# Layer 1's experts in a fused two-block model: tokens picked and results added by one-hot products instead of gathers and scatters

## The chip, the cores and the metric

The kernel runs on one core of a Trainium2 chip. The metric is the device time of one launch in microseconds. Everything is computed in f32. Engines: PE is TensorE (matrix products, accumulating in 8 PSUM banks of 128 x 512 f32), PEld its loads of the stationary operand, DVE is VectorE, ACT is ScalarE, POOL is GpSimd, SP only issues DMAs.

## The reference

256 tokens and 256 context tokens of width 1024 go through two layers of a first block (attention branches, gated merge, then a mixture of experts), and the 256 tokens through a second block (linear attention, short convolution, dilated attention, feed-forward). In layer 1 (the last of the first block) only the 256 tokens have experts. What matters here is the mixture:

```python
def hier_moe(x, w_group, b_group, w_router, b_router, w_gate, w_up, w_down):
    # x: 256 tokens in layer 1. One of 4 groups, then 2 of its 8 experts for each token
    top_w = softmax(top_l) * g_w              # a weight for each of the two
    ...
    def expert_block(args):                   # w_gate, w_up: 1024x512, w_down: 512x1024
        hdn = jax.nn.silu(xb @ w_gate[e]) * (xb @ w_up[e])
        return hdn @ w_down[e]
    ...
    return segment_sum(ys[dest] * w_sorted[:, None], order // TOP_K, num_segments=t)

h = h + gt2 * y.reshape(b, n_lat, D_MODEL)
```

32 experts of 3 x 2 MB of weights each make 201 MB per layer. In layer 1 they get 16 tokens each on average. A block has CAP = 64 places; tokens beyond that go into further blocks, which are run only if there are any.

## The kernel before, in words

**Weights.** SP issues all weight loads in one queue, in the order in which they are used. Each is a block of 128 x 4096 f32 (2,097,152 bytes) in one of eight slots: four of a ring, and four "homes" (parts of `branches`, `heads`, all of `xT`, all of `values`) that are free while experts run. A load waits until TensorE has read the slot's block before (`expert_read`). So SP is up to eight blocks ahead. The last two blocks come in four pieces each.

**Layout of an expert.** All 128 columns of TensorE are used for 64 tokens by halving the other side: rows 0 to 63 of a bank hold the first half of the outputs, rows 64 to 127 the second. `up_product` (L1342 in its loop) makes the gate product into S[b] and the up product into V[b], 16 products each of a stationary 128x64 tile of tokens on 256 columns of weights; the two halves go to different columns of the array. `down_product` (L1354) has 8 products on 512 columns. The b alternates from expert to expert, and so do nearly all buffers.

**Tokens.** ScalarE stores the normed tokens xn2 in DRAM (x_rows, L2126). For expert e+2 GpSimd gathers 64 half rows twice into `xg` by the table `token_of`; TensorE turns them with 4 transposes into A[1] (L1331), ScalarE copies that to `xgT`. Expert 0's tokens come without DRAM, by one-hot products (`first_rows`, L1318). The tables come from one-hot products too (`place_rows`, L1307).

**Hidden rows and result.** ScalarE takes silu of the gate product, VectorE multiplies by the up product (L3051), TensorE turns the hidden rows with 2 transposes into A[0], ScalarE copies them to `hidT`, the down product goes to V[2+b], VectorE scales it by the gate gt2 into `y_sb` (L3118), and GpSimd scatters it to y_rows in DRAM. The last two experts' results (`KEPT_EXP`) are kept in SBUF (`last_y`, L3110) and added by one-hot products that also hold the tokens' weights (`last_sum`, L892). At the end y_rows is read back, one row pair per token (`result`, `first_result`), weighed (`weigh_first`, L3155) and added to `h` together with the banks of `last_sum` (`combine`, L3165). Then `second_in` does two norms (L3189 to L3209), turns the rows (L1459) and starts the second block's first products (L1493).

**Order.** `turn` runs eight experts (`MOE_AHEAD`); the first and the last eight are written out, the middle 16 are two passes of a hardware loop on every engine. Between the loop and the last eight stand the further blocks: each engine steps over them one by one if there are none. In experts 1 to 5 of the first eight VectorE also counts and lists the further blocks and places the kept ones. TensorE's order for an expert is: gate product, up product, transposes of the next expert's tokens, transposes of the hidden rows, down product. `keep_going` (L1278) are products without use that keep TensorE busy.

**Around it.** Ahead of the experts stand `merge_out` (the attention part's last product with the norm and the router's logits, L1225 to L1252) and `route`: VectorE picks the experts, TensorE ranks the tokens in each expert (L1289 to L1292).

## Time and profile before

| | |
|---|---|
| median of 3 runs | 2649.85 us (2649.2 to 2654.93) |
| profiled execution, its own time | 2650.99 us |
| its span, first to last instruction | 2649.1 us |
| PE busy | 2451.3 us, 93% |
| PEld busy | 1568.9 us, 59% |
| DVE / ACT / POOL busy | 960.6 / 434.9 / 170.1 us |
| granted TensorE clock, mean | 0.993 |
| DMA | 666.63 MB, mean 252 GB/s |
| layer 1's experts | gate product of expert 0 at 1532.28 us, last down product from 1998.05 us |

Times are read on the span's own clock, in microseconds from its first instruction. A MATMUL group's time reaches to the modelled end of its last instruction, which overlaps the next group: for a pace, starts are compared with starts. An f32 product shows as two MATMULs, a transpose as one. "[0.69 <-ACT ...]" behind a group is the idle time before it and what ended it; "issue" means nothing that the profile shows.

### The profile page before, as it was taken

The numbers are of one execution on the slowest core, as the hardware profiler recorded it, in microseconds if no ns is written. First come the engines' busy times: TensorE is split into PE (matmuls) and PEld (weight loads), VectorE is DVE, ScalarE is ACT, GpSimd is POOL, SyncE is SP. The second block draws the span as 40 slices with busy tenths as digits, with TensorE's granted clock in tenths as the row PEclk, the third lists the DMA queues.
The fourth block names the chain that finished last, engine by engine and source line by source line (L and its number), as shares of the span: only waits on it lengthen the run. The fifth ranks groups of instructions, "written<-read, shape, count | busy, mean of one in ns | idle before, by whom it ended". The sixth has DMA issues, their size and how long they took to land.

```text
span 2649.1 us, 32934 instructions
## 1 busy us (share of the span) xinstructions
PE 2451.3 (93%) x13288; PEld 1568.9 (59%) x13288; DVE 960.6 (36%) x1959; ACT 434.9 (16%) x1040; POOL 170.1 (6%) x193
## 2 busy tenths in 40 slices
PE   8999999999987777799999999777879999999998
PEld 4444455565554444447878755434445778997983
DVE  2695454335311111156555421000003333554750
ACT  2121223201100000022132110000001222211110
POOL 0000000000111111100000012111110000000000
PEclk9999999999999999999999999999999999999999
DMA  8365010434999999965424699999996333344441
GB/s 334 146 259 199 32 65 32 159 127 188 410 425 426 425 427 425 418 270 222 190 96 159 253 399 421 424 425 426 425 419 245 138 117 114 126 158 161 163 172 48
DMA packets 63062, 666.63 MB, mean 252 GB/s; under 512 B 13058, under 2 KB 13346, under 8 KB 24400
## 3 DMA queue, kind: packets, MB, share of 16 engines
q1 hardware_dynamic: 48384, 634.68, 59.3%
q0 software_dynamic: 13392, 24.82, 2.5%
q10 hardware_dynamic: 1152, 5.24, 0.5%
q8 instruction: 97, 1.59, 0.2%
q14 instruction: 37, 0.30, 0.0%
HBM read 664.28 MB, written 21.02 MB: 259 GB/s over the span
## 4 chain that ended last, share of the span: by engine, by line
PE 71%; DMA 25%; ACT 1%; issue 1%; DVE 1%; SPq 0%; POOL 0%; DVEq 0%; ACTq 0%; POOLq 0%
DMA ring<-in_w_moe 11%; DMA values<-in_w_moe 8%; PE act_bank L822 5%; PE act_bank L835 5%; PE act_bank L1484 5%; PE vec_bank L1016 4%; PE vec_bank L1225 4%; PE score_bank L1000 4%; PE score_bank L1342 4%; PE vec_bank L1354 3%; PE vec_bank L1000 3%; PE score_bank L1172 3%; PE vec_bank L1342 3%; DMA xT<-in_w_moe 3%; PE act_bank L1172 2%; PE act_bank L1493 2%
## 5 line engine op out<-in xcount | busy, mean ns | idle before, releaser
L3051 DVE TENSOR_TENSOR heads<-work,vec_bank 128x256 f32<-128x256 f32 x64 | 26.9, 421 | 505.6 <-PE vec_bank L1342 505.6
L822 PE MATMUL act_bank<-ring,xT 128*128 128x512 f32 x352 | 154.6, 593 | 3.2 <-ACT work L1827 2.5
L1354 PE MATMUL vec_bank<-ring,heads 128*64 128x512 f32 x512 | 116.9, 597 | 28.1 <-DMA ring<-in_w_moe 18.5
L1342 PE MATMUL score_bank<-ring,branches 128*64 128x256 f32 x1024 | 120.8, 389 | 23.1 <-DMA ring<-in_w_moe 11.3
L1342 PE MATMUL vec_bank<-ring,branches 128*64 128x256 f32 x1024 | 119.0, 385 | 24.9 <-DMA ring<-in_w_moe 24.7
L835 PE MATMUL act_bank<-xT,ring 128*128 128x512 f32 (+1 forms) x384 | 138.6, 521 | 0.0
L1484 PE MATMUL act_bank<-xT,ring 128*128 128x256 f32 x576 | 126.6, 380 | 0.6 <-ACT work L2247 0.6
L1342 PEld LDWEIGHTS score_bank<-ring,branches 128*64 128x64 f32 x1024 | 80.7, 140 | 71.6 <-issue 41.0
L1016 PE MATMUL vec_bank<-branches,ring 128*128 128x256 f32 (+1 forms) x416 | 122.7, 445 | 0.0
L1484 PEld LDWEIGHTS act_bank<-xT,ring 128*128 128x128 f32 x576 | 108.7, 190 | 16.7 <-issue 2.2
L1342 PEld LDWEIGHTS vec_bank<-ring,branches 128*64 128x64 f32 x1024 | 76.3, 138 | 65.6 <-DMA ring<-in_w_moe 29.9
L822 PEld LDWEIGHTS act_bank<-ring,xT 128*128 128x128 f32 x352 | 65.7, 190 | 82.9 <-issue 82.9
L3581 POOL TENSOR_TENSOR stat<-stat,const 128x1 f32<-128x1 f32 (+3 forms) x35 | 23.6, 673 | 1400.6 <-DVE stat L2727 465.1
L1225 PE MATMUL vec_bank<-ring 128*128 128x512 f32 x256 | 111.7, 593 | 0.0
L835 PEld LDWEIGHTS act_bank<-xT,ring 128*128 128x128 f32 x384 | 72.7, 190 | 63.7 <-issue 60.3
L2146 ACT ACTIVATE work<-score_bank 128x256 f32<-128x256 f32 x64 | 24.6, 384 | 519.3 <-PE score_bank L1342 482.9
L2471 DVE CUSTOM_DVE_ANT_0 ring<-ring,branches 128x1024 f32<-128x1024 f32 x80 | 100.6, 1279 | 19.8 <-DMA ring<-in_w_ada 19.6
L3629 POOL DMA_INDIRECT y_rows<-work,table x60 | 61.0, 1017 | 707.9 <-DVE work L3118 678.9
L1000 PE MATMUL score_bank<-xT,ring 128*128 128x256 f32 (+1 forms) x320 | 106.1, 472 | 0.0
L1016 PEld LDWEIGHTS vec_bank<-branches,ring 128*128 128x128 f32 x416 | 78.0, 190 | 35.6 <-issue 28.7
L1827 ACT ACTIVATE branches<-act_bank 128x512 f32<-128x512 f32 (+1 forms) x70 | 40.9, 585 | 303.8 <-PE act_bank L1331 287.0
L1354 PEld LDWEIGHTS vec_bank<-ring,heads 128*64 128x64 f32 x512 | 37.2, 136 | 87.2 <-issue 63.3
(535 smaller groups left out, 3885.2 us busy)
## 6 DMA issues: line engine op xcount, KB each, us to landing
ring<-in_w_moe SPq DMA_DIRECT2D x95, 2048.0 KB
ring<-in_w_in SPq DMA_DIRECT2D x29, 2048.0 KB
ring<-in_w_merge SPq DMA_DIRECT2D x27, 2048.0 KB
branches<-in_w_moe SPq DMA_DIRECT2D x24, 2048.0 KB
heads<-in_w_moe SPq DMA_DIRECT2D x24, 2048.0 KB
ring<-in_w_ada SPq DMA_DIRECT2D x23, 2048.0 KB
values<-in_w_moe SPq DMA_DIRECT2D x23, 2048.0 KB
xT<-in_w_moe SPq DMA_DIRECT2D x22, 2048.0 KB, 36.7
```

The costliest lines, as they stand in the source:

```text
L822: mm = pe.matmul(b.t[:, :], xT[:, k, tile * P:(tile + 1) * P], w[:, k * COLS:(k + 1) * COLS], start=(k == 0), stop=(k == KD - 1))
L835: mm = pe.matmul(b.t[:, 0:n], w[:, k * COLS + f * P:k * COLS + (f + 1) * P], xT[:, k, 0:n], start=(k == 0), stop=(k == KD - 1))
L1000: mm = pe.matmul(g.t[:, 0:n], merge_tile(l, i, MERGE_TILES * d + k), xs[:, k, 0:n], start=(k == 0), stop=(k == KD - 1))
L1016: mm = pe.matmul(y.t[:, 0:n], merge_tile(l, i, MERGE_TILES * d + KD + k), ys[:, BRANCH_ORDER[i], k, 0:n], start=(k == 0), stop=(k == 3))
L1172: mm = pe.matmul(b.t[:, 0:n], w[:, k, :], x[:, k, :], start=(first and k == 0), stop=(k == KD // 2 - 1), skip_group_check=True)
L1225: mm = pe.matmul(b.t[:, :], merged[l][:, k, tile * P:(tile + 1) * P], w[:, k * COLS:(k + 1) * COLS], start=(k == 0), stop=(k == KD - 1))
L1342: mm = pe.matmul(o.t[g * CAP:(g + 1) * CAP, 0:D_HALF], xgT[:, b, c, half * CAP:(half + 1) * CAP], w[:, c0:c0 + D_HALF], start=(k == 0), st ...
L1354: mm = pe.matmul(o.t[g * CAP:(g + 1) * CAP, :], hidT[:, b, c, half * CAP:(half + 1) * CAP], w[:, c0:c0 + HALF], start=(k == 0), stop=(k == 3))
L1484: mm = pe.matmul(b.t[:, 0:SEQ], w[:, k * COLS + f * P:k * COLS + (f + 1) * P], x2T[:, k, :], start=(k == 0), stop=(k == KD - 1))
L1493: mm = pe.matmul(b.t[:, :], x2T[:, k, tile * P:(tile + 1) * P], w[:, k * COLS:(k + 1) * COLS], start=(k == 0), stop=(k == KD - 1))
L2471: ins = nc.vector.tensor_tensor_reduce(ada_junk if k < ns - 1 else w, w, cond_rows[:, k, :], 1.0, bias, ALU.mult, ALU.add, dst)
L3629: pool.indirect_dma_start(out=half_rows(y_rows[l][0:tiles(l) * 2 * P, :]), out_offset=bass.IndirectOffsetOnAxis(ap=table[:, e:e + 1], axis=0),
```

## The change

Only layer 1 is touched (and what follows it at once). xn2 stays in SBUF, now in `h[:, 2:4]`, which is free there. For each expert VectorE compares every token's slot number with 1 to 64 (`find_tokens`, a one-hot matrix of 256 tokens x 64 places) and multiplies that by the token's weight (`hold_tokens`). TensorE makes the expert's transposed tokens as xn2^T x one-hot (`tokens_product`) into A[1]. It turns hidden rows and weighed one-hot together (`turn_held`), and adds y to all 256 tokens by 4 products into the four V banks, which accumulate over all 32 experts (`add_to_tokens`). These come one expert later, between the next up product and transposes. All buffers are single: S[0] for gate product and turned rows, S[1], A[0], A[1], `xgT[:, 0]`, `hid[:, 0]`, `y_sb[:, 0]`. x_rows, y_rows, the tables and the gathers, scatters and results of layer 1 go. The diff, cut:

```diff
-    xn2 = [xhat, ring[SUMS][:, 2048:4096].rearrange("p (t n) -> p t n", t=2)]
+    xn2 = [xhat, h[:, 2:4, :]]
...
+            if l == DEPTH - 1:
+                pe.wait_ge(A[1].free, A[1].fills)
+                pe.wait_ge(hot_made.sem, 1)
+                tokens_product(hot_now, A[1]).then_inc(A[1].full, A[1].fill())
+                mark["first_tokens"] = at_bank(A[1])
+                return
...
+        def tokens_product(hot, o):
+            for k in range(KD):
+                half, c = k // (KD // 2), k % (KD // 2)
+                for tile in range(2):
+                    mm = pe.matmul(o.t[:, c * P + half * CAP:c * P + (half + 1) * CAP], xn2[DEPTH - 1][:, tile, k * P:(k + 1) * P],
+                                   hot[:, tile, :], start=(k == 0 and tile == 0), stop=(k == KD - 1 and tile == 1),
+                                   skip_group_check=True)
+            return mm
+
+        def turn_held(o, hidden_, held_):
+            for c in range(2):
+                pe.transpose(o.t[:, c * P:(c + 1) * P], hidden_[:, c * P:(c + 1) * P], ident)
+            for tile in range(2):
+                mm = pe.transpose(o.t[:, (2 + tile) * P:(3 + tile) * P], held_[:, tile].rearrange("p h n -> p (h n)"), ident)
+            return mm
+
+        def add_to_tokens(y, turned_, first=False, last=False):
+            for tile in range(2):
+                for g in range(2):
+                    rows, b = slice(g * CAP, (g + 1) * CAP), V[2 * tile + g]
+                    mm = pe.matmul(b.t[:, :], turned_[rows, 2 * P + tile * P:2 * P + (tile + 1) * P], y[rows, :],
+                                   start=first, stop=last, skip_group_check=True)
...
+        def held_expert(q, e, loaded, first=False, second=False, final=False):
...
+            pe.wait_ge(A[1].free, A[1].fills)
+            for r, o in ((0, S[0]), (1, S[1])):
+                split = final and r == 1
+                if not split:
+                    pe.wait_ge(ring_loaded[s[r]], loaded(r))
+                pe.wait_ge(o.free, o.fills)
+                up_product(o, 0, ring[s[r]], pieces_of(r) if split else None).then_inc(o.full, o.fill())
+            if not first:
+                pe.wait_ge(A[0].free, A[0].fills)
+                if second:
+                    emptied(*V)
+                add_to_tokens(y_sb[:, 0, :], turned_both, first=second)
+            pe.wait_ge(S[0].free, S[0].fills)
+            pe.wait_ge(S[1].free, S[1].fills)
+            pe.wait_ge(held_made.sem, e + 1)
+            turn_held(S[0], hid[:, 0, :], held).then_inc(S[0].full, S[0].fill())
+            if not final:
+                pe.wait_ge(A[1].free, A[1].fills)
+                pe.wait_ge(hot_made.sem, e + 2)
+                tokens_product(hot_now, A[1]).then_inc(A[1].full, A[1].fill())
+                pe.wait_ge(ring_loaded[s[2]], loaded(2))
+            pe.wait_ge(A[0].free, A[0].fills)
+            pe.wait_ge(S[0].free, S[0].fills)
+            down_product(A[0], 0, ring[s[2]], pieces_of(2) if final else None).then_inc(A[0].full, A[0].fill())
...
+        def held_expert(final=False):                                   # ScalarE
+            act.wait_ge(S[0].full, S[0].reads + 1)
+            act.wait_ge(S[1].free, S[1].reads)
+            nc.scalar.activation(silu_s[:, 0, :], S[0].t[:, 0:D_HALF], ACT.Silu).then_inc(S[0].free, S[0].read())
+            S[1].read()
+            evacuate(S[0], turned_both)
+            if not final:
+                evacuate(A[1], xgT[:, 0, :, :], shape=4)
...
+        def find_tokens(e):                                             # VectorE
+            if not isinstance(e, int) or e > 0:
+                dve.wait_ge(held_made.sem, e)
+            hot_tokens(hot_now, slot_numbers[:, 0:CAP], one_of(e)).then_inc(hot_made.sem, hot_made.up())
+
+        def hold_tokens(e):
+            dve.wait_ge(hot_made.sem, e + 1)
+            weighed_tokens(held, hot_now, one_of(e)).then_inc(held_made.sem, held_made.up())
...
+            if l == DEPTH - 1:                                          # route
+                step(STT(out=slot_of_token, in0=rank, scalar=1.0, in1=pick, op0=ALU.add, op1=ALU.mult))
+                find_tokens(0)
...
+        def held_expert(e):                                             # VectorE
+            l = DEPTH - 1
+            dve.wait_ge(S[1].full, S[1].seen + 1)
+            dve.wait_ge(S[0].free, S[0].seen + 1)
+            TT(hid[:, 0, :], silu_s[:, 0, :], S[1].t[:, 0:D_HALF], ALU.mult).then_inc(S[1].free, 1)
...
+            dve.wait_ge(A[0].full, mark["moe", l]["A"][0] + e + 1)
+            TT(y_sb[:, 0, :], A[0].t[:, :], gt2_halves[:, 0, :], ALU.mult).then_inc(A[0].free, 1)
+            if not isinstance(e, int) or e < N_EXP - 1:
+                hold_tokens(e + 1)
+            if not isinstance(e, int) or e < N_EXP - 2:
+                find_tokens(e + 2)
...
+        def add_held(tile):
+            for g in range(2):
+                half, b = slice(g * COLS, (g + 1) * COLS), V[2 * tile + g]
+                dve.wait_ge(b.full, b.reads + 1)
+                TT(h[:, tile, half], h[:, tile, half], b.t[:, :], ALU.add).then_inc(b.free, b.read())
...
-                combine(DEPTH - 1, tile)
+                add_held(tile)
...
-                if AT[c][0] == SUMS and l > 0:
-                    rows_taken(l)
...
-        result_behind = {("in", 1, "U"): (0, 1), ("in", 1, "V"): (0, 2), ("in", 1, "VA"): (0, 3),
-                         ("in2", 2, IN2_ORDER[0]): (1, 1)}
+        result_behind = {("in", 1, "U"): (0, 1), ("in", 1, "V"): (0, 2), ("in", 1, "VA"): (0, 3)}
```

## Rows read from the trace of the kernel before

**Rows 1.** Stretches: length, busy time by engine, granted clock, DMA share, GB/s.

```profile
1560.00:1600.00 40.00, 38.05 (x287) 24.45 (x285) 10.33 (x34) 3.77 (x9) 7.95 (x8) 1.00 1.01 424
...
1634.00:1876.00 242.00, 189.56 (x1364) 101.06 (x1360) 17.80 (x32) 20.17 (x48) 34.98 (x36) 0.99 1.01 425
...
2100.00:2200.00 100.00, 100.00 (x499) 71.87 (x498) 37.07 (x76) 20.02 (x50) 0.00 (x0) 1.00 0.34 127
```

**Rows 2.** The chain of waits: start, length, what (L1172 has 128 columns here).

```profile
1445.11 0.89 PE act_bank L1172 x8
...
1713.85 38.60 DMA ring<-in_w_moe
...
1992.77 15.13 DMA heads<-y_rows
```

**Rows 3.** TensorE in order of time: expert 7, and two later gate products.

```profile
1622.12 3.65 PE L1342 MATMUL score_bank<-heads,branches 128*64 128x256 f32 x32
...
1629.16 0.66 PE L1331 MATMUL act_bank<-const,branches 128*128 128x128 f32 x4
...
1630.87 3.65 PE L1354 MATMUL vec_bank<-ring,heads 128*64 128x512 f32 x16 [0.69 <-ACT heads L1827]
1634.32 3.65 PE L1342 MATMUL score_bank<-ring,branches 128*64 128x256 f32 x32
...
1710.00 3.67 PE L1342 MATMUL score_bank<-ring,branches 128*64 128x256 f32 x32 [1.27 <-DMA ring<-in_w_moe]
...
1973.04 3.67 PE L1342 MATMUL score_bank<-values,branches 128*64 128x256 f32 x32 [1.30 <-issue]
```

**Rows 4.** All engines in order of time, from routing to expert 1.

```profile
1527.85 0.29 DVE L2963 TENSOR_TENSOR heads<-const,work 128x128 f32<-128x128 f32 x1
...
1528.19 1.94 PE L1318 MATMUL act_bank<-ring,heads 128*64 128x512 f32 x8
...
1532.28 3.67 PE L1342 MATMUL score_bank<-ring,branches 128*64 128x256 f32 x32
...
1547.56 0.66 PE L1331 MATMUL act_bank<-const,branches 128*128 128x128 f32 x4 [1.76 <-DMA branches<-x_rows,token_of]
...
1548.90 3.67 PE L1342 MATMUL score_bank<-ring,branches 128*64 128x256 f32 x32 [0.69 <-ACT branches L1827]
```

**Rows 5.** In order of time, TensorE at the router's logits (36 columns).

```profile
1517.66 0.66 PE L1240 MATMUL act_bank<-const,ring 128*128 128x128 f32 x4 [0.73 <-DVE ring L2888]
1518.15 1.93 PE L1252 MATMUL vec_bank<-wr,xT 128*128 128x36 f32 x16
...
1519.92 7.11 PE L1278 MATMUL vec_bank<-const 128*128 128x256 f32 x24
```

**Rows 6.** In order of time, TensorE at last_sum of tile 1.

```profile
2005.11 1.99 PE L892 MATMUL vec_bank<-work 64*128 64x512 f32 x8
...
2007.03 1.56 PE L1278 MATMUL vec_bank<-const 128*128 128x256 f32 x6
```

**Rows 7.** In order of time, TensorE from the last up product to the second block.

```profile
1995.48 1.08 PE L1342 MATMUL vec_bank<-xT,branches 128*64 128x256 f32 x8 [0.16 <-DMA xT<-in_w_moe]
...
1997.09 0.44 PE L1331 MATMUL act_bank<-const,heads 128*128 128x128 f32 x2 [0.52 <-DVE heads L3051]
...
1998.05 3.65 PE L1354 MATMUL vec_bank<-ring,heads 128*64 128x512 f32 x16 [0.52 <-issue]
...
2001.63 2.05 PE L892 MATMUL vec_bank<-work 64*128 64x512 f32 x8
...
2010.66 10.54 PE L1493 MATMUL act_bank<-ring,xT 128*128 128x512 f32 x24 [0.33 <-issue]
```

**Rows 8.** TensorE behind the loop in order of time, and a stretch (columns of Rows 1, with L1342 alone, PE and PEld).

```profile
1882.36 0.66 PE L1405 MATMUL act_bank<-const,work 128*128 128x128 f32 x2 [2.64 <-issue]
...
1884.17 6.05 PE L1342 MATMUL score_bank<-ring,branches 128*64 128x256 f32 x32
...
1884.00:1890.00 6.00, 5.83 (x32) 3.43 (x34) 0.58 1.02 425
```

More of the change, by code:

```diff
@@ new lines, in turn_held @@
+        def turn_held(o, hidden_, held_):
[10 more added lines that the diff above has]
+                                   start=first, stop=last, skip_group_check=True)
+                    if last:
+                        mm.then_inc(b.full, b.fill())
+                        mark["added", DEPTH - 1, tile, g] = let_go(b)
+            return mm
@@ new lines, in held_experts, with loads @@
+        def held_experts():
+            l = DEPTH - 1
+            n_turn = N_EXP // MOE_AHEAD
+            def loads(q, r, i):
+                return 16 * (AT["expert", l, 3 * q + r][1] + 1) + 48 * i
+            mark["moe", l] = {"S": [b.fills for b in S], "A": [b.fills for b in A]}
+            for q in range(MOE_AHEAD):
+                held_expert(q, q, lambda r: loads(q, r, 0), first=(q == 0), second=(q == 1))
+            turns = Turns((S[0], "fills", 2 * MOE_AHEAD), *[(b, "fills", MOE_AHEAD) for b in (S[1], A[0], A[1])])
+            with pe.Fori(1, n_turn - 1) as i:
+                turns.turn(i - 1)
+                for q in range(MOE_AHEAD):
+                    held_expert(q, MOE_AHEAD * i + q, lambda r: loads(q, r, i))
+            turns.done(n_turn - 2)
+            mark["moe_late", l] = at_bank(A[0])
+            with further_blocks(pe, l) as j:
+                s = xb[l]
+                emptied(*A, *S)
+                pe.wait_ge(s["index"], j + 1)
+                tokens_product(hot_more, A[1]).then_inc(s["pe"], 1)
+                pe.wait_ge(s["act"], 3 * j + 1)
+                pe.wait_ge(s["weights"], 48 * j + 48)
+                up_product(S[0], 1, ring[0])
+                up_product(S[1], 1, ring[1]).then_inc(s["pe"], 1)
+                pe.wait_ge(s["gate"], j + 1)
+                pe.wait_ge(s["dve"], 2 * j + 1)
+                turn_held(S[0], hid[:, 1, :], held_more).then_inc(s["pe"], 1)
+                pe.wait_ge(s["act"], 3 * j + 3)
+                down_product(A[0], 1, ring[2], None, turned_more[:, 0:2 * P].rearrange("p (k n) -> p k n", k=2))\
+                    .then_inc(s["pe"], 1)
+                pe.wait_ge(s["dve"], 2 * j + 2)
+                add_to_tokens(y_sb[:, 1, :], turned_more).then_inc(s["pe"], 1)
+            for q in range(MOE_AHEAD):
+                last = n_turn - 1
+                held_expert(q, MOE_AHEAD * last + q, lambda r: loads(q, r, last), final=(q == MOE_AHEAD - 1))
+            mark["moe_end", l] = at_bank(A[0])
+            pe.wait_ge(A[0].free, A[0].fills)
+            add_to_tokens(y_sb[:, 0, :], turned_both, last=True)
@@ L1797, in _ @@
             route(l)
-            experts(l)
+            if l < DEPTH - 1:
+                experts(l)
+            else:
+                held_experts()
         second_in()
@@ new lines, in held_experts @@
+        def held_experts():
+            l = DEPTH - 1
+            between = {1: count_further, 2: place_further, 3: list_further}
+            for b in range(2):
+                S[b].seen = mark["moe", l]["S"][b]
+            for q in range(MOE_AHEAD):
+                held_expert(q)
+                if q in between:
+                    between[q](l)
+            last = N_EXP // MOE_AHEAD - 1
+            turns = Turns((S[0], "seen", 2 * MOE_AHEAD), (S[1], "seen", MOE_AHEAD))
+            with dve.Fori(1, last) as i:
+                turns.turn(i - 1)
+                for q in range(MOE_AHEAD):
+                    held_expert(MOE_AHEAD * i + q)
+            turns.done(last - 1)
+            with further_blocks(dve, l) as j:
+                s, r = xb[l], r_area[l]
+                e = dve.value_load(r["x_list"][:, bass.ds(2 * j + 1, 1)], min_val=0, max_val=N_EXP - 1)
+                c = dve.value_load(r["x_list"][:, bass.ds(2 * j + 2, 1)], min_val=0, max_val=SEQ - CAP)
+                hot_tokens(hot_more, slot_numbers[:, bass.ds(c, CAP)], bass.ds(e, 1)).then_inc(s["index"], 1)
+                dve.wait_ge(s["index"], j + 1)
+                weighed_tokens(held_more, hot_more, bass.ds(e, 1)).then_inc(s["gate"], 1)
+                dve.wait_ge(s["act"], 3 * j + 2)
+                TT(hid[:, 1, :], silu_s[:, 1, :], S[1].t[:, 0:D_HALF], ALU.mult).then_inc(s["dve"], 1)
+                dve.wait_ge(s["pe"], 5 * j + 4)
+                TT(y_sb[:, 1, :], A[0].t[:, :], gt2_halves[:, 0, :], ALU.mult).then_inc(s["dve"], 1)
+                dve.wait_ge(s["pe"], 5 * j + 5)
+                dve.sem_inc(s["passed"], 1)
+            for q in range(MOE_AHEAD):
+                held_expert(MOE_AHEAD * last + q)
@@ L3551, in _ @@
             route(l)
-            experts(l)
+            if l < DEPTH - 1:
+                experts(l)
+            else:
+                held_experts()
         second_in()
```

131 lines of the change are left out of this document (104 added, 27 removed).

## The prediction

> **What bounds the kernel now.** I read the stretches of the span first, then the chain of waits, then single instructions. While layer 1's experts run, the 16 DMA engines are full: from 1634 to 1876 us their share is 1.01 at 425 GB/s, and TensorE is busy for only 189.56 of 242 us [rows 1]. In the chain of waits nearly all of this stretch is weight DMA, in pieces like the 38.60 us one at 1713.85 [rows 2]. The start is different: from 1560 to 1600 us TensorE is busy for 38.05 of 40 us [rows 1], because eight blocks of weights were loaded ahead. One expert takes TensorE 1634.32 - 1622.12 = 12.20 us there; with the weights awaited, 17 experts take 1973.04 - 1710.00 = 263.04 us, 15.47 each [rows 3]. So TensorE has 3.27 us to spare per expert, and this is what the change spends. After the layer, from 2100 to 2200 us, TensorE is busy for all 100 us [rows 1]: a delay of the layer's end is not made good there.
>
> The profiled execution took 2650.99 us: a span of 2649.1 and 1.89 around it. It is 1.14 us above the median of the three runs (2649.85). I work on the span, and quote the result against the median.
>
> **The change on TensorE, one expert in steady state.** A matrix product of f32 shows as two instructions, a transpose as one.
> - The gate and up products are as before: from the start of the first to the start of the transposes 1629.16 - 1622.12 = 7.04 us [rows 3].
> - add_to_tokens is new: 4 products of 64 rows by 128 columns on 512, 8 instructions. The kernel before has just this in last_sum, with the same alternation of upper and lower rows: 2007.03 - 2005.11 = 1.92 us [rows 6].
> - turn_held has four transposes (two of the hidden rows, two of the held weights). Before there were two of the hidden rows and four of the tokens. Four take 1518.15 - 1517.66 = 0.49 us [rows 5].
> - tokens_product is new: 8 x 2 = 16 products, 32 instructions, each with a stationary tile of 128x128 and only 64 moving columns. The trace has no such form, so I bound it by its neighbours: with 36 columns 16 instructions take 1519.92 - 1518.15 = 1.77 us, 0.111 each [rows 5]; with 128 columns 8 take 0.89 us, 0.111 each [rows 2]. The pace doesn't depend on the columns below 128, so 64 must cost the same: 32 x 0.111 = 3.54 us. From below: two products of 256 columns side by side come at 0.108 per instruction (3.46 / 32, [rows 3]), that is 0.42 ns a column, so 64 columns of a full-width product (twice 64) can't take less than 0.054 each, 1.7 us in all. I take 3.45, near the rows of both neighbours.
> - The down product: 1634.32 - 1630.87 = 3.45 us [rows 3].
>
> The sum is 7.04 + 1.92 + 0.49 + 3.45 + 3.45 = 16.35; I take 16.4 for one more change of form. With the switches of form left out it is 15.9, with 3.54 and a switch of 0.1 at each new border 16.6.
>
> A rule of the Trainium skill speaks for more. The trace shows 0.111 us per instruction at 36 and at 128 moving columns [rows 2, 5]. "TensorE: Matmul & The Clock Gate", section on packing small matmuls, says that a weight load overlaps a running matmul only if it goes to another row group, and its section on LDWEIGHTS gives columns / 1.2 ns, an estimate of 107 ns for 128. By this rule a pair would cost 107 + 54 = 161 ns and tokens_product 5.1 us. The 128-column row contradicts it (it would be 107 + 107 there).
>
> **What TensorE waits for.** In the early stretch before, 0.6 to 0.7 us per expert was spent between the transposes and the down product. In the new order each wait has cover:
> - hid: from the end of the up product to the transposes a bare wait takes 1997.09 - (1995.48 + 8 x 0.108) = 0.75 us [rows 7]; add_to_tokens covers it with 1.92. Without that cover it would be +0.75 per expert.
> - Evacuating the turned bank (512 columns) takes 1548.90 - 1547.56 = 1.34 from the first transpose [rows 4], so 0.85 after the last; tokens_product covers it.
> - Evacuating the new tokens is as long and lies beside the down product; scaling y lies beside the next expert's 7 us.
> - VectorE: find_tokens is as large as the 0.29 us operation at 1527.85 [rows 4], hold_tokens twice as wide, so at most 0.6. Both come an expert ahead; behind them on the queue is only the next hid, some 6 us later. The small operations that count and list further blocks in experts 1 to 3 fit there too.
>
> **DMA.** Three blocks of 2,097,152 bytes are 6.29 MB, at 425 GB/s 14.8 us; with its gathers and scatters an expert took 15.47. Without them it lies between 14.8 and 15.47. Either is under 16.4, so from the second expert on TensorE is the bound, and what the removed DMAs free is worth nothing. The loads stay in order on the sync queue, eight blocks ahead; the eighth no longer waits for the first rows and can only come earlier. The stores of x_rows, two memsets and the index tables lay beside other work and cost nothing before.
>
> **Start.** slot_of_token and the first hot tile replace the two operations ahead of the first product: its start moves from 1528.19 to about 1528.25 [rows 4]. Then 3.45 for tokens_product and 1.34 - 0.43 = 0.91 until the gate product may start: 1532.6, against 1532.28 before [rows 4]. Expert 0: 6.9 + 0.75 (uncovered, nothing to add yet) + 0.49 + 3.45 + 3.45 = 15.05, so expert 1 begins at 1547.7. Before it was 1548.90, after a wait for the first gather: 1.2 us gained.
>
> **End.** Experts 1 to 30: 30 x 16.4 = 492, to 2039.7. Expert 31 has no tokens_product to cover the evacuation: 7.04 + 1.92 + 1.34 + (2001.63 - 1998.05 = 3.58) = 13.9, to 2053.6. Leaving the loop after expert 23 costs TensorE a gap of "issue" before: 2.64 us at 1882.36 [rows 8], bare of any DMA, where the skipped further blocks are stepped over. It stays, with 0.2 around it: 2.8. After it the granted clock was 0.58 in 1884 to 1890 (most of it at 1.2 instead of 2.4 GHz) after TensorE had stood idle, and the gate product took 6.05 instead of 3.65 [rows 3, 8]: 2.4 us. Before, another wait of 0.56 followed the gap and goes now, so the drop may or may not come: 0 to 2.4, I take 1.2. The jump back of the loop after expert 15 hid in a DMA wait: 0 to 1.3, I take 0.5. The last down product then ends at 2053.6 + 2.8 + 1.2 + 0.5 = 2058.1, where it was 2001.63 [rows 7]: 56.5 later.
>
> From there to the second block's first long product is 2010.66 - 2001.63 = 9.03 us before [rows 7]. The same steps remain (y, four products of which two are needed first, sum, squares, power, transposes), at the same lengths. The chain names the result's DMA from DRAM, 15.13 us at 1992.77 [rows 2], ahead of a power on GpSimd; but in the code that power waits for VectorE's value alone, and GpSimd's wait for y_in[1] stands behind it. So taking the DMA away shortens nothing here. Tile 1 loses its wait for rows and one weighing, 2.6 us beside TensorE at full load: nothing. So 0 to -0.5 here.
>
> **Forecast.** 2649.1 + 56.5 = 2705.6 span; with 1.89, and less the 1.14 to the median, 2706. Its own range: 15.9 to 16.6 per expert is -15 to +6, the clock and the loop -1.7 to +2: 2692 to 2714.
>
> **Rivals.**
> - *The stationary load is not hidden* (161 ns a pair): tokens_product costs 5.1 us, 1.65 more, 31 times: +51, 2757. For it: nothing but that 64 columns leave less to hide behind. Against: the 36-column row leaves even less and runs at 0.111. Chance 0.04.
> - *The single buffers leave a wait open* (one bank S[0] for both the gate product and the turned rows, one xgT, one y_sb): a wait of 0.75 to 1.3 per expert is exposed, +23 to +40, about 2737. Against: every cover above is over twice the wait. Chance 0.06.
> - *The two halves of add_to_tokens do not run side by side*: 3.4 instead of 1.7, +53, 2759. Against: last_sum has the same form. Chance 0.02.
> - *Other side: the narrow products are as cheap as their columns*, 1.7 us instead of 3.45. Then an expert costs TensorE 14.7, under the 14.8 to 15.47 of its weights; the weights stay the bound and the removed rows count: up to 0.67 us for 23 experts, 15 us earlier, 2635. It decides from 3.45 - (16.4 - 15.1) = 2.15 us, 0.067 per instruction. For it: the banks and the half-width products go at the speed of their columns. Against: both rows at 0.111. Chance 0.04.
>
> **How the numbers follow.** The forecast has 0.84. A measurement of this kernel tells apart about 0.2%, 5 us. Faster is the last rival and a little for a miscounted bound: 0.05; within 0.2% 0.01; slower 0.94. The range is that of the forecast, a little wider above for part of an open wait: 2692 to 2718.
>
> **What would show it.** Per expert, gate product to gate product: 16.4 us in the new trace. tokens_product at 3.4 to 3.55, add_to_tokens at 1.9. DMA share in the stretch at about 14.8 / 16.4 = 0.9 and no weight wait on TensorE; the sync queue waiting for TensorE instead. TensorE idle under 0.5 us per expert. It is wrong if TensorE still waits for weights, or if the pace is under 15.5 or above 17.

## The result and the profile after

The changed kernel takes 2725.88 us (median of four, 2723.91 to 2730.29) against 2649.86 (four, 2649.2 to 2654.93): ratio 1.029, interval 1.0277 to 1.0302. The forecast was 2706 with a range to 2718, so the kernel is 20 us above the forecast and 8 above the range. The direction is as predicted, and so is what bounds the experts; two of the forecast's terms are not. The profiled execution has a span of 2724.3 us, 75.2 more than before where the working gave 56.5: 18.7 us are missing, which the rest of this section places.

The page of the changed kernel: busy time by engine, the DMA total, the chain by engine, and the group of `tokens_product`.

```profile
PE 2594.5 (95%) x14468; PEld 1684.8 (62%) x14468; DVE 966.0 (35%) x1981; ACT 443.3 (16%) x1037; POOL 105.3 (4%) x130
...
DMA packets 57462, 659.56 MB, mean 242 GB/s; under 512 B 9008, under 2 KB 9296, under 8 KB 19040
...
PE 85%; DMA 11%; issue 1%; DVE 1%; ACT 1%; SPq 0%; POOL 0%; DVEq 0%; ACTq 0%
...
L1378 PE MATMUL act_bank<-work,h 128*128 128x64 f32 x1024 | 117.9, 273 | 0.2 <-DVE work L3077 0.2
```

Stretches of the changed kernel (columns of [rows 1]): the steady state, where before the DMA share was 1.01 and TensorE had idle time; and the two edges of TensorE's hardware loop.

```profile
1540.00:1670.00 130.00, 130.00 (x978) 81.22 (x977) 18.47 (x51) 12.02 (x23) 2.18 (x4) 1.00 0.94 380
1790.00:1806.00 16.00, 10.37 (x52) 4.74 (x52) 1.31 (x3) 0.62 (x2) 0.00 (x0) 0.81 0.61 232
1930.00:1960.00 30.00, 22.37 (x149) 13.90 (x150) 1.74 (x4) 2.17 (x4) 0.00 (x0) 0.89 0.70 281
```

In the first line TensorE is busy for all 130 us and the DMA share is down to 0.94: the bound has moved from the weights to TensorE. In the other two TensorE stands idle for 5.6 and 7.6 us, at a lower clock in the rest, and the DMA share falls too, since the loads wait for TensorE. These two places are most of the miss.

One expert in steady state, TensorE in order of time, answering to [rows 3]:

```profile
1545.80 7.08 PE L1355 MATMUL score_bank<-ring,branches 128*64 128x256 f32 x64
1552.81 1.99 PE L1396 MATMUL vec_bank<-work,heads 64*128 64x512 f32 x8
1554.72 0.44 PE L1386 MATMUL score_bank<-const,heads 128*128 128x128 f32 x2
1555.00 0.38 PE L1388 MATMUL score_bank<-const,work 128*128 128x128 f32 x2
1555.22 3.68 PE L1378 MATMUL act_bank<-work,h 128*128 128x64 f32 x32
1558.83 3.65 PE L1369 MATMUL act_bank<-heads 128*64 128x512 f32 x16
1562.31 3.62 PE L1355 MATMUL score_bank<-xT,branches 128*64 128x256 f32 x32
```

Start to start: gate and up 7.01 us, `add_to_tokens` 1.91, `turn_held` 0.50, `tokens_product` 3.61 (0.113 per instruction), down 3.48: 16.51 in all, with no idle time between them.

The jump back of the loop, between experts 15 and 16, and the exit behind expert 23, with the skipped further blocks:

```profile
1790.05 3.65 PE L1369 MATMUL act_bank<-ring,heads 128*64 128x512 f32 x16
1796.95 3.40 PE L1355 MATMUL score_bank<-ring,branches 128*64 128x256 f32 x16 [3.25 <-issue]
1802.72 3.13 PE L1355 MATMUL score_bank<-ring,branches 128*64 128x256 f32 x16 [2.38 <-issue]
1805.63 4.18 PE L1355 MATMUL score_bank<-branches 128*64 128x256 f32 x32
1809.74 1.99 PE L1396 MATMUL vec_bank<-work,heads 64*128 64x512 f32 x8
...
1931.37 3.65 PE L1369 MATMUL act_bank<-ring,heads 128*64 128x512 f32 x16
1942.66 5.65 PE L1355 MATMUL score_bank<-ring,branches 128*64 128x256 f32 x32 [7.63 <-issue]
1948.12 3.63 PE L1355 MATMUL score_bank<-branches 128*64 128x256 f32 x32
1951.69 1.99 PE L1396 MATMUL vec_bank<-work,heads 64*128 64x512 f32 x8
```

Without an edge, `add_to_tokens` follows a down product after 3.48 + 7.04 = 10.52 us. At the jump it comes after 19.69 and at the exit after 20.32: 9.2 and 9.8 us lost. Each has two parts: "issue" gaps, in which TensorE waits for nothing that the profile shows, and products at a lower clock behind them (16 instructions in 3.40 us where 32 take 3.6; 32 in 5.65).

The sum on the spans:

| | forecast | measured |
|---|---|---|
| start of expert 1 | 1547.7 | 1545.80 (-1.9) |
| experts 1 to 30 | 30 x 16.4 | 30 x 16.51 (+3.3) |
| jump back | 0.5 | 9.2 (+8.7) |
| exit | 4.0 | 9.8 (+5.8) |
| last down product ends | 2058.1 | 2074.2 (+16.1) |
| from there to the second block's long product | 9.03 | 8.95 (-0.1) |
| second block | as before, 638.4 | 641.1 (+2.7) |

56.5 + 16.1 - 0.1 + 2.7 = 75.2. The two edges are 14.5 us of the 18.7. The last term has one visible part of 1.7 us: the first long product runs at a lower clock for a while, 12.23 us instead of the 10.54 of [rows 7], and TensorE stood idle for 1.92 us ahead of it. The other 1.0 is no more than the traces differ by: in those where this product takes 10.54, the second block takes 638.4 to 641.1 us.

```profile
2081.73 0.66 PE L1585 MATMUL score_bank<-const,branches 128*128 128x128 f32 x4 [1.92 <-DVE branches L3470]
...
2083.15 12.23 PE L1619 MATMUL act_bank<-ring,xT 128*128 128x512 f32 x24 [0.33 <-issue]
```

### The profile page after: what moved, and what is told of

Read it like the earlier page. It is cut to its first block, busy times and chain, and to the rows that moved or that the text cites. A ratio compares the mean times of both kernels' runs of the same rounds, so it can differ in the third digit from the quotient of the medians.

```text
span 2724.3 us, 35211 instructions
## 1 busy us (share of the span) xinstructions
PE 2594.5 (95%) x14468; PEld 1684.8 (62%) x14468; DVE 966.0 (35%) x1981; ACT 443.3 (16%) x1037; POOL 105.3 (4%) x130
## 3 DMA queue, kind: packets, MB, share of 16 engines
q10 hardware_dynamic: 720, 3.15, 0.3%
## 4 chain that ended last, share of the span: by engine, by line
PE 85%; DMA 11%; issue 1%; DVE 1%; ACT 1%; SPq 0%; POOL 0%; DVEq 0%; ACTq 0%
PE score_bank L1355 10%; DMA values<-in_w_moe 8%; PE act_bank L829 6%; PE act_bank L842 5%; PE act_bank L1610 5%; PE vec_bank L1023 4%; PE act_bank L1369 4%; PE act_bank L1378 4%; PE vec_bank L1232 4%; PE score_bank L1007 4%; PE vec_bank L1007 3%; PE score_bank L1179 3%; DMA xT<-in_w_moe 3%; PE act_bank L1179 2%; PE vec_bank L1396 2%; PE act_bank L1619 2%
## 5 line engine op out<-in xcount | busy, mean ns | idle before, releaser
L1355 PE MATMUL score_bank<-ring,branches 128*64 128x256 f32 x1536 | 179.8, 390 | 25.0 <-issue 19.6
L1355 PEld LDWEIGHTS score_bank<-ring,branches 128*64 128x64 f32 x1536 | 116.5, 141 | 94.7 <-issue 47.9
L3373 DVE TENSOR_TENSOR work<-act_bank,work 128x512 f32<-128x512 f32 x32 | 22.1, 692 | 287.7 <-PE act_bank L1369 287.7
L1378 PE MATMUL act_bank<-work,h 128*128 128x64 f32 x1024 | 117.9, 273 | 0.2 <-DVE work L3077 0.2
L1378 PEld LDWEIGHTS act_bank<-work,h 128*128 128x128 f32 x1024 | 116.9, 192 | 0.6 <-issue 0.6
L3263 DVE TENSOR_TENSOR heads<-work,vec_bank 128x256 f32<-128x256 f32 x32 | 13.5, 421 | 253.3 <-PE vec_bank L1355 253.3
L1007 PE MATMUL vec_bank<-xT,ring 128*128 128x512 f32 (+1 forms) x256 | 86.7, 487 | 0.0
L1232 PEld LDWEIGHTS vec_bank<-ring 128*128 128x128 f32 x256 | 48.1, 190 | 57.0 <-issue 56.9
L3367 DVE TENSOR_TENSOR heads<-work,score_bank 128x256 f32<-128x256 f32 x32 | 13.5, 421 | 193.8 <-PE score_bank L1355 193.8
```

The lines of the kernel that those rows point to most:

```text
L1007: mm = pe.matmul(g.t[:, 0:n], merge_tile(l, i, MERGE_TILES * d + k), xs[:, k, 0:n], start=(k == 0), stop=(k == KD - 1))
L1232: mm = pe.matmul(b.t[:, :], merged[l][:, k, tile * P:(tile + 1) * P], w[:, k * COLS:(k + 1) * COLS], start=(k == 0), stop=(k == KD - 1))
L1355: mm = pe.matmul(o.t[g * CAP:(g + 1) * CAP, 0:D_HALF], xgT[:, b, c, half * CAP:(half + 1) * CAP], w[:, c0:c0 + D_HALF], start=(k == 0), st ...
L1378: mm = pe.matmul(o.t[:, c * P + half * CAP:c * P + (half + 1) * CAP], xn2[DEPTH - 1][:, tile, k * P:(k + 1) * P], hot[:, tile, :], start=( ...
```

## The experiments

Kernels are shown as their edit to the changed kernel unless said otherwise. "The edges" are the jump back and the exit of TensorE's loop in layer 1.

### Are the edges the missing time?

**written_out**: TensorE's loop written out (the other engines keep theirs).

```diff
-            with pe.Fori(1, n_turn - 1) as i:
+            for i in range(1, n_turn - 1):
```

> The changed kernel with TensorE's loop over experts 8 to 23 of layer 1 written out (only TensorE's; all other engines keep theirs). Theory A, instructions: the 9.2 us lost around the loop's jump back (gate product of expert 16 late by 3.4, a gap of 2.4 inside it, the rest at half clock) are TensorE's own instructions not being there after a jump. Then they go: about 2717 us, and the exit's 9.8 us stay. Rival B, another engine's or SP's own jump makes TensorE wait: nothing changes, 2726.

**no_further**: layer 1 has no further blocks on any engine, so nothing is skipped at the exit (leaves out experts with more than 64 tokens, of which this data has none).

```diff
+        if l == DEPTH - 1:
+            return
         with eng.Fori(0, further(l)) as j:
```

> The changed kernel without layer 1's further blocks on any engine (with these inputs none of the seven runs; leaving them out gives up the case of an expert with over 64 tokens). Theory A: stepping over seven skipped bodies costs TensorE the 7.8 us gap after expert 23 and 2.0 us at half clock behind it; both go, about 2716, and the jump back's 9.2 stay. If the gap is the loop's exit itself, or weights that come late there, it stays: 2726.

**both_edges**: both edits together.

> Both of these together: TensorE's loop written out and no further blocks in layer 1. Theory A: all of 19 us go, 2707, which is what 16.5 us per expert gives without edges (my forecast was 2706, with 4.5 us for both edges). If the two edges share one cause that only moves, it is above 2715.

**short_body**: the six steps in the body of TensorE's further block (which never runs) become single transposes; the loop and its skipping stay.

> The changed kernel with all seven further blocks, but TensorE's body cut to six transposes (62 products before; the body never runs with these inputs, and would compute nothing of use). If the cost of stepping over is that of fetching far past a long body, the gap of 7.8 us shrinks to about that of the kernel before (2.8): 2719. If it is a price per iteration, whatever the body holds, it stays: 2726.

Measured, against 2649.85 for the kernel before:

| | us | ratio |
|---|---|---|
| written_out | 2711.97 | 1.0237 [1.022, 1.0254] |
| no_further | 2717.18 | 1.0255 [1.0238, 1.0272] |
| both_edges | 2707.56 | 1.0217 [1.02, 1.0234] |
| short_body | 2721.17 | 1.0264 [1.0247, 1.0281] |

With both edges away the changed kernel takes 18.3 us less, about the 19.0 read from its trace. It lands near the forecast of 2706, but that has luck in it: the forecast had 4.5 us for the edges, so without them it would have been 2701.5, and the 6 us above that are about what the table has for the rest (experts +3.3, second block +2.7, start -1.9). Written out, the jump costs nothing. Without further blocks the exit costs nothing and the jump has gaps of 3.17 and 2.02 us. The exit is no fixed price: where the loop is written out, the same full bodies are skipped in 2.69 us, and the gate product behind runs at full clock. So written_out came out 5 us under its expectation, which had left the exit its 9.8 us (2.9 are left). With the short body the gap is 2.81 us, the loss 3.0. In no_further, written_out and short_body, TensorE in order of time (first line: behind the jump; the other two: behind the exit):

```profile
1797.43 3.48 PE L1356 MATMUL score_bank<-ring,branches 128*64 128x256 f32 x16 [3.17 <-issue]
```

```profile
1927.32 3.67 PE L1355 MATMUL score_bank<-ring,branches 128*64 128x256 f32 x32 [2.69 <-issue]
```

```profile
1943.05 3.67 PE L1355 MATMUL score_bank<-ring,branches 128*64 128x256 f32 x32 [2.81 <-issue]
```

### Were the edges there before, and what do freed DMAs buy?

**before_edges**: the kernel before, with the edits of both_edges.

> The kernel before with TensorE's loop of layer 1 written out and no further blocks in layer 1 (the case of over 64 tokens given up). Theory: there the same edges lie under the wait for weights, of which eight blocks are ahead, so taking them away is worth nothing: 2647 to 2651. If the edges cost time there too, it is 2640 or less.

Measured 2651.48 against 2650.74, ratio 1.0003 [0.9993, 1.0013]. In the kernel before the edges are worth nothing: what the exit costs (the gap of 2.64 us in [rows 8]) was covered by the wait for weights, and the jump is taken up below.

**cut_tokens**: both_edges, and `tokens_product` makes only one of its 8 column blocks per expert (leaves out 7/8 of the tokens' columns).

> The changed kernel without its two edges (loop written out on TensorE, no further blocks) and with only 2 of the 16 products of tokens_product from the second expert on; it leaves out seven eighths of the tokens' columns. TensorE then needs 16.5 - 3.6 + 0.45 + some 0.4 of uncovered evacuation = 13.8 us per expert. Theory: the weights become the bound again at 14.8 to 15.1 us per expert and the removed rows count, 2635 to 2642. If something besides TensorE's work per expert holds the new order (its single buffers, the single queue), it stays above 2660.

Measured 2631.48, ratio 0.992 [0.9904, 0.9935], 3.5 us under the expected range. TensorE then needs 13.85 us per expert, less than the weights. It goes at that pace on the blocks loaded ahead until about 1844 us and at 14.7 us per expert from 1858 on; the DMA engines are full all the time, and the weights bound again:

```profile
1700.00:1900.00 200.00, 192.00 (x1370) 117.15 (x1368) 24.50 (x57) 20.57 (x42) 0.00 (x0) 1.00 1.01 427
```

So the DMAs removed, with the earlier start of expert 1, are worth some 19 us, but only to a kernel in which TensorE is not the bound; `tokens_product` costs more than that.

**gathered**: tokens are stored, gathered and turned as in the kernel before (4 transposes instead of 32 instructions), results are added in the four V banks as in the changed one. All is computed. TensorE's held_expert:

```diff
+            if not final and not first:
+                turn_tokens((q + 1) % 2, gathers)
...
-                tokens_product(hot_now, A[1]).then_inc(A[1].full, A[1].fill())
```

> A mix of both kernels: tokens of layer 1 are stored and gathered as before (and turned with 4 transposes, 0.5 us, in place of tokens_product's 3.6), results are added in the four V banks as in the changed kernel, so no scatters, no result rows in DRAM, no last_sum. It computes everything. TensorE: 7.0 + 1.9 + 0.5 + 0.5 + 0.4 + 3.5 = 13.8 us per expert, less than the weights' 14.8 to 15.1. Theory: bound by weights, with 2.1 MB of scatters and 1 MB of result rows less in front of the last block (3.1 MB at 425 GB/s = 7.5 us): 2642. If the edges' 9 us each do not fit under the eight blocks ahead, up to 10 us more. Rival: the order with single buffers costs more than it seems, 2660.

**gathered_written_out**: gathered, with TensorE's loop written out.

> The same mix with TensorE's loop written out (further blocks kept). If the jump back is hidden under the weights in the mix, it is the same within 2 us; if it is not, up to 9 us faster than the mix with the loop.

Measured 2643.78, ratio 0.9966 [0.9952, 0.9979], and 2646.95, 0.9979 [0.9968, 0.999]. The half of the change that takes results out of DRAM is a gain of 0.3%: it takes the scatters off the bound, and an early expert takes TensorE 13.85 us for 12.20 before, 1.65 of the 3.27 that it had to spare. The weights stay the bound:

```profile
1640.00:1870.00 230.00, 220.46 (x1555) 117.35 (x1555) 27.81 (x64) 24.61 (x50) 17.04 (x17) 1.00 1.01 425
```

Writing the loop out buys nothing. This looked like cover by the weights again, but the trace of gathered has no gap at all at the jump (down product 1751.12, gate product 1754.60). That led to the last question.

**gathered_kept_busy**: gathered with `keep_going(10, A[1])` instead of 6 ahead of the second block.

> The mix of gathered tokens and results added in banks (all blocks and loops kept), with 10 instead of 6 products without use on TensorE while the first tile is normed after the last expert. In the mix TensorE stood idle for 1.91 us there and the second block's first long product then took 12.23 us instead of the kernel before's 10.54. If the idle time is what let the clock fall, the product takes 10.5 again and the whole is 1.7 us faster than the mix, 2642 (within the scatter of its runs; the trace tells). If the clock falls anyway, 12.2.

Measured 2642.35, ratio 0.997 [0.9958, 0.9982], not to be told from gathered. In its trace the idle time is gone and the long product takes its 10.54 us again. First gathered, then this kernel:

```profile
1998.73 0.66 PE L1580 MATMUL score_bank<-const,branches 128*128 128x128 f32 x4 [1.91 <-DVE branches L3460]
...
2000.15 12.23 PE L1614 MATMUL act_bank<-ring,xT 128*128 128x512 f32 x24 [0.33 <-issue]
```

```profile
1997.80 0.66 PE L1580 MATMUL score_bank<-const,branches 128*128 128x128 f32 x4 [0.19 <-DVE branches L3460]
...
1999.22 10.54 PE L1614 MATMUL act_bank<-ring,xT 128*128 128x512 f32 x24 [0.33 <-issue]
```

That the idle time is what took the clock down isn't shown by this. Fourteen traces have the same gap of 1.91 or 1.92 us at this place; behind it the long product takes 11.49 to 12.23 us in eleven of them, but 10.54 in three (one_further, body_3, body_1). So one trace at 10.54 without the gap may be chance. In one_further:

```profile
2076.40 0.66 PE L1585 MATMUL score_bank<-const,branches 128*128 128x128 f32 x4 [1.91 <-DVE branches L3470]
...
2077.82 10.54 PE L1619 MATMUL act_bank<-ring,xT 128*128 128x512 f32 x24 [0.33 <-issue]
```

### Why does the exit cost what it does?

**one_further**: the loop over further blocks has one iteration instead of seven to skip, with its full body.

```diff
-        with eng.Fori(0, further(l)) as j:
+        with eng.Fori(0, further(l) if l < DEPTH - 1 else 1) as j:
```

> The changed kernel with room for one further block in layer 1 instead of seven (with these inputs none runs); its body has full length. In the trace of the changed kernel two pieces of 16 KB of instructions came in the 7.6 us gap behind expert 23, with short bodies one and a gap of 2.8. If the gap is the price of the pieces, one long body still needs two: gap 5 us or more, about 2723. If it is a price per iteration stepped over (7 x 1.1 us), the gap is 1.1 us and the time 2717, as without further blocks.

Measured 2718.86, ratio 1.0257 [1.0241, 1.0273]. The gap is 2.51 us and the loss 4.6:

```profile
1937.62 5.14 PE L1355 MATMUL score_bank<-ring,branches 128*64 128x256 f32 x30 [2.51 <-issue]
```

A price per iteration is ruled out: one iteration gives a gap of 2.51 us, seven give 2.69 (written_out), 2.81 (short_body) or 7.63. The expectation that one long body needs two pieces of instructions was wrong as well: one piece comes in the gap (at 1935 us), the next at 1941, when TensorE has been at work again for over 3 us. What goes with the gap is how many pieces (see the next section) arrive before TensorE goes on. In the kernels with the new order it is two in each of the long gaps and one in each of the short ones:

| | exit's gap | pieces before TensorE goes on | loss |
|---|---|---|---|
| changed | 7.63 | 2 (1935, 1941) | 9.8 |
| body_6 | 8.78 | 2 | 10.9 |
| body_4 | 8.87 | 2 | 11.0 |
| body_2 | 8.48 | 2 | 11.6 |
| written_out | 2.69 | 1 (1924; the next at 1931) | 2.9 |
| short_body | 2.81 | 1 | 3.0 |
| one_further | 2.51 | 1 (1935; the next at 1941) | 4.6 |
| body_3, body_1, gathered | 2.87, 2.96, 2.96 | 1 | 4.8 to 4.9 |

The loss is the time from the down product to `add_to_tokens` above that of an expert without an edge; beside the gap it holds what the clock costs behind it. The kernel before had its gap of 2.64 us with no piece in it (its one piece came at 1887, behind the gap), so a fetch is not the whole price of the exit.

### Why does the jump back cost 9.2 us here and nothing in gathered?

In the profile the DMAs that bring instructions stand in queues of their own. TensorE's are in q8, in pieces of 16 KB: from body_3 to body_2, whose kernels differ in TensorE's code alone, it is q8 that changes. In the second pass of the loop, the changed kernel (1806 to 1930) has seven of them:

```profile
DMA packets 3159, 46.24 MB, mean 373 GB/s; under 512 B 337, under 2 KB 337, under 8 KB 337
## 3 DMA queue, kind: packets, MB, share of 16 engines
q1 hardware_dynamic: 3152, 46.12, 92.2%
q8 instruction: 7, 0.11, 0.4%
```

The kernel before (1762 to 1880) has none: what the first pass fetched was still there.

```profile
DMA packets 4614, 50.24 MB, mean 426 GB/s; under 512 B 1226, under 2 KB 1226, under 8 KB 1652
## 3 DMA queue, kind: packets, MB, share of 16 engines
q1 hardware_dynamic: 3334, 48.53, 96.9%
q0 software_dynamic: 1280, 1.71, 3.9%
```

A loop body of eight experts is 8 x 2 x 86 = 1376 products and weight loads before, 8 x 2 x 96 = 1536 in gathered, 8 x 2 x 124 = 1984 in the changed kernel. The theory: a body up to some length is kept, a longer one is fetched again in each pass, and the first pieces after the jump are not there in time. The experiment makes the body shorter and leaves both edges as they are: `tokens_product` makes n of its 8 column blocks (leaves out the other columns of the tokens), 16 instructions less per expert for each two blocks.

```diff
-                tokens_product(hot_now, A[1]).then_inc(A[1].full, A[1].fill())
+                tokens_product(hot_now, A[1], n).then_inc(A[1].full, A[1].fill())
```

> The changed kernel with both edges of the loop as they are, but tokens_product makes only 6 of its 8 column blocks per expert in steady state (leaves out a quarter of the tokens' columns). It tests the length of TensorE's loop body. In the changed kernel TensorE's instructions come at one 16 KB piece per 16.0 us in the first pass (15 in 1540 to 1780), 1.03 per expert, so the body of eight experts is 8.2 pieces; 7 come again in the second pass (1806 to 1930). In the kernel before the body is 5.6 pieces by the same count (9 in 186 us, 12.9 experts), and none come from 1762 to 1880; in the gathered kernel (6.3 pieces) none at the jump back, and no gap. Theory A: TensorE keeps a body up to some length between 6.3 and 8.2 pieces and jumps back free; a longer one is fetched again, 3 pieces on demand, 9.2 us. This body is 8 x 16 instructions shorter, 7.7 pieces: if the limit is 8, no gap and 0 to 1 pieces in the second pass. Rival B: the jump costs this whatever the body's length: 3 pieces and gaps of about 3.2 and 2.4 us stay. TensorE needs 16.51 - 8 x 0.113 = 15.6 us per expert: 2725.9 - 31 x 0.9 = 2698 with the gap, 2689 without.

> As body_6 with 4 of 8 column blocks (leaves out half of the tokens' columns). The body is 8 x 32 instructions shorter than the changed kernel's, 7.2 pieces. Theory A (too long a body is fetched again): now it should be short enough: no gap behind the down product at the jump back, at most one piece there, and 0 to 1 pieces in the second pass where the changed kernel has 7. Rival B (the jump itself, whatever the length): 3 pieces and gaps of about 3.2 and 2.4 us as before. Time: TensorE 16.51 - 16 x 0.113 = 14.7 us per expert, just under the weights' 14.8 to 15.0, so the weights bound most of it and hide part of any edge: 2640 to 2655 by A, up to 5 more by B.

> The changed kernel with 3 of 8 column blocks in tokens_product in steady state (leaves out five eighths of the tokens' columns). TensorE's loop body counts 8 x 2 x 104 = 1664 products and weight loads, against 1984 in the changed kernel, 1728 with 4 blocks (both fetched again in the second pass), 1536 in the gathered kernel (no piece at the jump back). By length alone (theory A) the limit lies between 1536 and 1728, so this one is open: either as with 4 blocks (2 to 3 pieces at the jump, a gap of about 3, 7 pieces in the second pass) or none of it. By rival B (the jump in the changed kernel costs pieces whatever the body's length) as with 4 blocks. Time about 2640 to 2655 with the weights as the bound.

> As body_3 with 2 of 8 column blocks: 1600 products and loads in the body. Theory A: probably no piece and no gap at the jump back, none or one in the second pass, if the limit is above 1600; otherwise as with 4 blocks. Rival B: 2 to 3 pieces at the jump and 7 in the second pass. Time 2635 to 2645.

> As body_3 with 1 of 8 column blocks: 1536 products and loads in the body, just as many as in the gathered kernel, where no piece came at the jump back and the gap was nothing. Theory A must see the same here: down product to gate product 3.5 us at the jump, no piece there, at most one in the second pass. Rival B: 2 to 3 pieces at the jump, 6 to 7 in the second pass, and gaps that the wait for weights hides in part. Time 2630 to 2640, as in the kernel with both edges away and one block (2631.48).

| | instructions in the body | gaps at the jump | time lost there | pieces from the jump to the exit |
|---|---|---|---|---|
| changed | 1984 | 3.25, 2.38 | 9.2 | 10 |
| body_6 | 1856 | 3.22 | 3.4 | 9 |
| body_4 | 1728 | 2.98, 3.08 | 10.0 | 9 |
| body_3 | 1664 | 3.15 | 4.7 | 9 |
| body_2 | 1600 | none | 0 | 0 |
| body_1 | 1536 | none | 0 | 0 |
| gathered | 1536 | none | 0 | 0 |
| before | 1376 | a wait for weights | | 1, at the jump |

"Instructions" are TensorE's products and weight loads. The step lies between two neighbours that differ by 64 of them in 1600. Body_6, and body_4 after it, had been expected to be short enough already; the limit lies lower than I had put it. At the jump body_3, and then body_2, TensorE in order of time:

```profile
1756.75 3.65 PE L1369 MATMUL act_bank<-ring,heads 128*64 128x512 f32 x16
1763.56 5.01 PE L1355 MATMUL score_bank<-ring,branches 128*64 128x256 f32 x32 [3.15 <-issue]
```

```profile
1747.08 3.65 PE L1369 MATMUL act_bank<-ring,heads 128*64 128x512 f32 x16
1750.57 3.62 PE L1355 MATMUL score_bank<-ring,branches 128*64 128x256 f32 x32
```

And the second pass (DMA queues) of body_3, 1770 to 1880, where the whole body comes again, and of body_2, 1750 to 1860:

```profile
q1 hardware_dynamic: 3224, 46.88, 100.3%
q8 instruction: 7, 0.11, 0.4%
```

```profile
DMA packets 3236, 47.14 MB, mean 429 GB/s; under 512 B 359, under 2 KB 359, under 8 KB 359
## 3 DMA queue, kind: packets, MB, share of 16 engines
q1 hardware_dynamic: 3236, 47.14, 100.7%
```

The times: body_6 2696.36, ratio 1.0165 [1.0148, 1.0182], where its expectation had 2698 with the jump's gap; body_4 2670.42, 1.0075 [1.0056, 1.0094]; body_3 2648.03, body_2 2635.26 and body_1 2629.18 in one run each, with before at 2650.36. body_4 missed its range of 2640 to 2655: I had let the weights hide the edges, but at 14.73 us per expert TensorE was as much the bound as they were (100.00 of 100 us busy from 1600 to 1700 us, at a DMA share of 1.01), and both edges count in full. The rival, that the jump costs this whatever the body's length, is ruled out. The edit also shortens the code ahead of the loop, so where the loop begins within a piece moves along; no run moved it alone.

By the Trainium skill, "Advanced Engine Details and Errata", section ISA Cache, instructions are kept in lines of 16 KB or 256 instructions, on TensorE 128 KB in all. The pieces agree (0.11 MB in seven). In the changed kernel fifteen come from 1546 to 1778 us, one per 16.5 us or about one per expert: 248 products and loads, which by the Trainium skill's 256 leaves some 8 others. By that estimate the body of body_2 is 6.5 pieces long and that of body_3 6.8, while 128 KB would hold eight. This doesn't say that fewer than eight can be kept: a body that begins inside a piece touches more pieces than its length, and TensorE also fetches ahead.

## Why the prediction was wrong

- **The bound moves to TensorE, the weights become hidden**: right. DMA share 0.94 (forecast about 0.9), the sync queue waits for TensorE, and no wait for weights is left on TensorE.
- **16.4 us per expert**: right to 0.11, 3.3 us in all. `tokens_product` took 3.61 us where I took 3.45; the 3.54 of the neighbours' rows would have been nearer. `add_to_tokens`, `turn_held` and the down product are within 0.03.
- **Covers for the single buffers, the start, the tail**: right (no wait inside an expert; 1.9 us earlier; 8.95 for 9.03).
- **Leaving the loop, 4.0 us, and the jump back, 0.5 us**: this is the step that failed. They measured 9.8 and 9.2. The prediction read the exit's gap of 2.64 us [rows 8] as its price and put the jump back at "0 to 1.3", hidden in a DMA wait. By body_2, body_1 and gathered it was free for another reason than that cover: a body this short is still there in the second pass. The change itself lengthened the body from 1376 to 1984 instructions, over the limit, and that I did not count. At the exit the gap grew from 2.64 to 7.63 us: in the changed kernel TensorE goes on only when two pieces have come (at 1935 and 1941 us), where in the kernel before none came in the gap. The clock behind it cost 2.0 us where I took 1.2 (it fell in the kernel before too, [rows 8]). So the forecast had 4.5 us for the two edges, and they measured 19.0.
- **The second block as before**: off by 2.7 us, of which 1.7 are a product at a lower clock; the rest is within what the traces differ by.
- **Rivals**: none happened. The narrow product is neither cheap (3.61, not 1.7) nor does it pay for the load of its stationary tile on top (0.113 us for a load and its product together, not 0.161); the single buffers leave no wait; the halves of `add_to_tokens` run side by side (1.91 us, not 3.4). By the rule of the Trainium skill that was weighed there, the sum would have been 51 us higher; the trace contradicts it at 64 columns too.
- **The range** was made of terms that the trace showed. Nothing in it stood for a cost that appears only when code grows. (Its own terms, -15 and -1.7, give 2689 for the lower end, not 2692.)

What stays open: why TensorE has to wait for a second piece at the exit in some kernels (gaps of 7.63 to 8.87 us: changed, body_6, body_4, body_2) and not in others (2.5 to 3.0 us: written_out, short_body, one_further, body_3, body_1, gathered). It goes neither with the length of the loop's body nor with the number of skipped iterations. Where the code behind the blocks falls within a piece may decide it; that is not shown, since no run moved the code without changing it. Nor is it known why the jump costs 3.4 us in body_6 and 10.0 in body_4, with the same nine pieces in the second pass.

## What to carry to other kernels

Count the instructions in a hardware loop's body before and after a change, and look in the trace whether its second pass fetches instructions: a body that crosses the limit turns a free jump into one that costs 3.4 to 10.0 us here, and no row of the old trace shows it. When a change spends an engine's slack, all that was hidden in the slack comes out at once; price each such place by itself. And take a change apart: here the half that used little of the bound-to-be engine (results in banks) gains 0.3%, the other half loses 3%.

## What the runs showed of the hardware

- TensorE keeps a loop body of 1600 products and loads (1536 and 1376 as well) and fetches one of 1664 or more again in each pass: none against seven pieces of 16 KB. Steady fetching costs nothing (130 us of 130 busy at one piece per 16.5 us). In the changed kernel the first three pieces after the jump come at 1794, 1800 and 1804 us, and TensorE waits for the first two.
- The length of an idle gap doesn't tell whether the clock falls behind it. Gaps of 1.91 us were followed by 12.23 us for a product of 10.54 in gathered and by 10.54 in one_further; gaps of 2.69, 2.81 and 3.22 us (the exits of written_out and short_body, the jump of body_6) by a gate product of 3.67 us, gaps of 2.87 and 2.96 (the exits of body_3 and body_1) by one of 5.36.
- An f32 product of a 128x128 stationary tile costs 0.113 us per instruction with 64 moving columns, next to 0.111 with 36 and with 128.
